# Another issue order for the differential attention, with the second chunk's copy on VectorE

## The reference

```
h   = rms_norm(x);  P = h @ w_in               # split into the q, k, v of two mixers
A   = sliding-window attention, window 128, learned sinks
B   = differential attention: 4 heads, two softmax maps each, chunk-causal over all keys
x   = x + rms_norm(concat(A, B) @ w_out)
x   = x + rms_norm((silu(h2 @ w_gate) * (h2 @ w_up)) @ w_down)

# B, for one block of 128 query rows of one head:
sc = q[m] @ k[m].T / 8, masked;   p[m] = softmax(sc)      # m = 0, 1
o  = (p[0] - lam * p[1]) @ v;     o = rms_norm(o) * g * (1 - lambda_init)
```

## Time and profile before

| what | value |
|---|---|
| median of three runs | 2519.32 us |
| profiled execution, its own time | 2519.68 us |
| its span, first to last instruction | 2517.9 us |
| TensorE busy over the span | 2369.7 us (94%) |
| VectorE, ScalarE, GpSimd busy over the span | 1591.8, 1218.6, 680.0 us |
| B: first score block to last norm | 630.5 to 1015.4 us |

### The profile page before, as it was taken

One profiled execution on the slowest core, in us unless ns is written; L12 is line 12 of the kernel. 1 busy time (PEld: TensorE's weight loads), 2 busy tenths in 40 slices (PEclk: granted clock), 3 DMA queues, 4 the chain that ended last, 5 costly groups with the idle time before them and its releaser, 6 DMA issues.

```text
span 2517.9 us, 34871 instructions
## 1 busy us (share of the span) xinstructions
PE 2369.7 (94%) x11796; PEld 1972.9 (78%) x11796; DVE 1591.8 (63%) x3045; ACT 1218.6 (48%) x2779; POOL 680.0 (27%) x810
## 2 busy tenths in 40 slices
PE   6999987997899999799999999999999999999997
PEld 5888876885778778577778888888888888888886
DVE  5677775554788888333664654657786455465877
ACT  5555564332677777433443333345454333334444
POOL 1233322221576676355511101100001111111001
PEclk9999998998899999899999999999999999999999
DMA  5111112433332231567552322256764332226774
GB/s 172 53 45 55 57 61 84 139 131 111 123 113 71 86 94 35 189 205 256 189 182 103 111 101 101 89 192 227 246 243 140 108 109 97 101 94 247 240 259 142
DMA packets 222354, 340.08 MB, mean 135 GB/s; under 512 B 20577, under 2 KB 119905, under 8 KB 220385
## 3 DMA queue, kind: packets, MB, share of 16 engines
q1 hardware_dynamic: 222176, 337.86, 39.8%
HBM read 234.50 MB, written 103.28 MB: 134 GB/s over the span
## 4 chain that ended last, share of the span: by engine, by line
PE 53%; POOL 2%; DVE 1%; issue 1%; ACT 1%; DMA 1%; SPq 0%; POOLq 0%; DVEq 0%; ACTq 0%
PE ff_psum L2444 33%; PE ff_psum L2468 17%; PE ff_psum L1722 3%; DMA op_w_raw<-in_w_out_dram 1%; PE ff_psum L1736 1%; POOL op_mt_lo L1507 0%; DVE op_h_row L1659 0%; DVE op_y_norm L1651 0%; POOL op_odd L1544 0%; POOL op_odd L1541 0%; ACT op_odd L1606 0%; DMA ff_hop<-hop_s 0%; DVE ff_y L2408 0%; ACT op_w_hi L1621 0%; POOL op_x_rstd L165 0%
## 5 line engine op out<-in xcount | busy, mean ns | idle before, releaser
L2444 PE MATMUL ff_psum<-ff_hop,ff_a_hi 128*128 128x512 f32 x2464 | 760.1, 390 | 3.7 <-DVE ff_hop L2208 2.8
L2444 PEld LDWEIGHTS ff_psum<-ff_hop,ff_a_hi 128*128 128x128 f32 x2464 | 463.0, 188 | 100.5 <-issue 5.0
L2444 PE MATMUL ff_psum<-ff_hop,ff_a_lo 128*128 128x512 f32 x1232 | 480.1, 390 | 0.0
L2444 PEld LDWEIGHTS ff_psum<-ff_hop,ff_a_lo 128*128 128x128 f32 x1232 | 231.6, 188 | 48.4
L2468 PE MATMUL ff_psum<-ff_a_hi 128*128 128x512 f32 x616 | 239.8, 389 | 0.0
L2468 PE MATMUL ff_psum<-ff_a_hi,ff_a_lo 128*128 128x512 f32 x616 | 239.7, 389 | 0.0
L2468 PE MATMUL ff_psum<-ff_a_lo,ff_a_hi 128*128 128x512 f32 x616 | 239.6, 389 | 0.0
L2074 ACT ACTIVATE ff_a_hi<-ff_w_raw 128x512 fp32r<-128x512 f32 x220 | 137.9, 629 | 194.2 <-PE ff_psum L2444 191.2
L2201 DVE TENSOR_TENSOR ff_a_lo<-ff_w_raw,ff_a_hi 128x512 fp32r<-128x512 f32 x220 | 163.4, 745 | 90.4 <-ACT ff_a_hi L2074 90.4
L1207 ACT ACTIVATE da_probs<-da_psum,da_bias 128x512 f32<-128x512 f32 (+3 forms) x320 | 195.7, 624 | 50.8 <-DVE da_bias L1259 45.8
L2029 POOL TENSOR_TENSOR ff_go<-ff_go 128x512 f32<-128x512 f32 x22 | 28.4, 1291 | 655.1 <-DVE ff_go L2282 635.2
(11 more groups left out here) (230 smaller groups left out, 4983.9 us busy)
## 6 DMA issues: line engine op xcount, KB each, us to landing
g_s<-ff_go SPq DMA_DIRECT2D x154, 256.0 KB, 2.0
ff_ring<-g_s SPq DMA_DIRECT2D x154, 256.0 KB, 2.7
ff_ring<-in_w_down_dram SPq DMA_DIRECT2D x132, 256.0 KB, 3.1
ff_w_raw<-in_w_gate_dram SPq DMA_DIRECT2D x44, 512.0 KB, 3.3
ff_w_raw<-in_w_up_dram SPq DMA_DIRECT2D x44, 512.0 KB, 3.4
pp_x<-in_x_dram SPq DMA_DIRECT2D x32, 512.0 KB, 4.3
ff_hop<-hop_s SPq DMA_DIRECT2D x14, 1024.0 KB, 7.8
hop_s<-op_odd SPq DMA_DIRECT2D x8, 1280.0 KB, 5.4
```

The lines of the kernel that those rows point to most:

```text
L2444: last = pe.matmul(ps[:, bank, :], w[:, unit % R, at], hop[i][:, h, c, :], start=(i in (0, 1, 6) and c == 0 and x_ == 0), stop=(c == 3 and ...
```

## The change

Four things differ, all in B. First, the shifts in `KINDS` and the durations that the planner assumes are other numbers; so is what an output scaling P must come after. Second, `COPIED_BY` gives chunk 1 to VectorE (G) in place of ScalarE (H). Third, three heads are planned in place of four, and the order of the third, seams included, is used for every head; events of the second head that fall behind the start of the third are marked as belonging to the head before ("ago" 1). Fourth, the wait of B on the factor is written for chunk 1 by number, which is the same chunk.

```
-    "S": ("PE", (-2.39, -1.12)),
+    "S": ("PE", (-1.33, -1.82)),
...
-COPIED_BY = ("H", "H", "H", "G")
+COPIED_BY = ("H", "G", "H", "G")
...
-    for h in range(DH):
+    for h in range(heads):
...
-                    us=1.85 * part[c] + 0.25 if combine == "A" else 0.98 * part[c] + 0.1)
+                    us=1.75 * part[c] + 0.3 if combine == "A" else 0.56 * part[c] + 0.1)
...
-            add("P", h, s, us=0.3, after=[("V", h, s, n - 1), second_last[0] >= 0 and ("N", *second_last)])
+            add("P", h, s, us=0.25, after=[("V", h, s, n - 1)])
...
-    order = sorted(start, key=lambda e: start[e])
+    begin = start["S", heads - 1, 0, 0, 0]
+    late = {(kind, *rest) for (kind, h, *rest), t in start.items() if h == heads - 2 and t >= begin}
+    order = []
+    for kind, h, *rest in sorted(start, key=lambda e: start[e]):
+        if h == heads - 2 and (kind, *rest) in late:
+            order.append((1, kind, *rest))
+        elif h == heads - 1 and (kind, *rest) not in late:
+            order.append((0, kind, *rest))
...
-            for kind, h, *rest in order:
-                perform(h, kind, *rest)
+            for event in order:
+                if event[0] == 0:
+                    perform(0, *event[1:])
+            for h in range(1, DH):
+                for ago, *event in order:
+                    perform(h - ago, *event)
+            for ago, *event in order:
+                if ago:
+                    perform(DH - 1, *event)
```

More of the change, by code:

```diff
@@ L912 @@
 KINDS = {
-    "S": ("PE", (-2.39, -1.12)),
[L914 to L926, removed]
+    "S": ("PE", (-1.33, -1.82)),
+    "R": ("DVE", (-0.33, 0.02)),
+    "M": ("DVE", (-1.55,)),
+    "E": ("ACT", (1.72, -2.49)),
+    "C": ("DVE", (-2.37,)),
+    "A": ("POOL", (0.0,)),
+    "B": ("DVE", (1.29,)),
+    "T": ("PE", (0.04,)),
+    "H": ("ACT", (0.17,)),
+    "G": ("DVE", (0.17,)),
+    "V": ("PE", (1.59,)),
+    "P": ("DVE", (1.31,)),
+    "Q": ("ACT", (-0.38,)),
+    "N": ("POOL", (1.3,)),
 }
 COMBINED_BY = ("A", "B", "A", "B")
-COPIED_BY = ("H", "H", "H", "G")
+COPIED_BY = ("H", "G", "H", "G")
 def attention_plan():
@@ L939, in attention_plan @@
     steps = len(chunks)
-    hop, own = 0.16, 0.05
+    heads, hop, own = 3, 0.16, 0.06
     events, turns = {}, {kind: [] for kind in KINDS}
@@ L958, in attention_plan @@
                 for c in range(n):
-                    add("S", h, s, m, c, us=max(0.455 * part[c], 0.28) + 0.03, after=[slot("E", "S", S_SLOTS)])
-                    add("R", h, s, m, c, us=0.53 * part[c] + (0.21 if c == n - 1 else 0.13), after=[("S", h, s, m, c)])
-                add("M", h, s, m, us=0.1, after=[("R", h, s, m, c) for c in range(n)])
+                    add("S", h, s, m, c, us=max(0.43 * part[c], 0.32), after=[slot("E", "S", S_SLOTS)])
+                    add("R", h, s, m, c, us=0.53 * part[c] + (0.34 if c == n - 1 else 0.07), after=[("S", h, s, m, c)])
+                add("M", h, s, m, us=0.08, after=[("R", h, s, m, c) for c in range(n)])
                 for c in range(n):
@@ L964, in attention_plan @@
                         after=[("M", h, s, m), second_last[0] >= 0 and ("T", *second_last, chunks[second_last[1]] - 1)])
-            add("C", h, s, us=0.46, after=[("E", h, s, m, c) for m in range(2) for c in range(n)])
+            add("C", h, s, us=0.6, after=[("E", h, s, m, c) for m in range(2) for c in range(n)])
             for c in range(n):
@@ L1009, in diff_attn @@
     ordinal, total = {}, {}
-    for kind, _, *rest in sorted(e for e in order if e[1] == 0):
-        ordinal[(kind, *rest)] = total[kind] = total.get(kind, 0) + 1
+    for _, *e in sorted(order, key=lambda e: (e[2], e[0])):
+        ordinal[tuple(e)] = total[e[0]] = total.get(e[0], 0) + 1
     S_BANKS, T_BANKS, O_BANK = range(S_SLOTS), range(S_SLOTS, S_SLOTS + T_SLOTS), S_SLOTS + T_SLOTS
@@ L1275, in perform @@
                         cols = slice(4 * P * c, 4 * P * c + width(s, c))
[L1276 removed]
+                        if c == 1:
                             dve.wait_ge(factor_ready, h * steps + s + 1)
```

10 lines of the change are left out of this document (5 added, 5 removed).

## The result

The changed kernel takes 2537.61 us (median of 4 runs, 2535.62 to 2540.92) against 2519.50 (2518.02 to 2520.41): ratio 1.0074, 95% interval 1.0056 to 1.0091, 18.1 us slower.

What follows compares the result with a forecast made beforehand. No engine is full: four hand work round in a ring, with 22.5 us of each 93.60 us head GpSimd's alone. 1.2 us a head, 4.8 in all, added to 2519.68 gave 2524.5 us; 8-in-10 range 2515 to 2537.

Steps and rivals of the forecast that it cites:

- B is closed: Attention stage: its gain or loss reaches the kernel one for one; no stage outside changes by more than 0.5 us.
- The sum of 1.2 us a head: Whole head, four times: slip of 1.2 us each, 4.8 in all; own range 0.5 to 2.5, chance 0.45.
- The seam, 0.95: Change of head: N11 ahead of A13 waits for late P11, making A14 0.95 us late; GpSimd keeps it through its stretch.
- Step 6, M6.0 1.2 late: VectorE, step 6: M6.0 moves behind R6.03 and R6.10, starting 1.2 us later, and the exponentials with it.
- Step 7, the copies ahead of M7.1, 1.4: VectorE, step 7: G6.1 and G6.3 add 0.93 us to 0.5, so M7.1 is 1.4 late; C7 slips 1.2.
- Step 8, G7.1 ahead of M8.1: VectorE, step 8: 0.60 us copy makes M8.1, C8 and T8.0 1.8 late; TensorE's saved 0.4 leaves S9.13 1.4 late.
- Steps 9 to 11: Later steps: copies go into VectorE's idle time, TensorE saves some 0.2 us, T11.0 is 1.2 late.
- The copies at nothing: VectorE copies in the GpSimd stretch (G12.1, G13.1, G2.1), or in front of an R waiting for scores, cost nothing.
- B beside A, taken as none: Combinations on VectorE beside A on GpSimd: could cost -0.8 to +0.8 us a step in four steps; taken as none.
- A (the seam absorbs): Rival: GpSimd's stretch starts when it did, losses inside a head vanish; -0.4 to +0.3 us a head, 2519.5 us, chance 0.22.
- B is out: Rival: TensorE's order decides and is faster, 1.3 us a head, 2514.5 us, if C8 slips under 0.5; chance 0.13.
- C, half of the copies pushing: Rival: VectorE becomes the bound; all copies 2545.3 us, half 2532.5; from half upward and what lies between, chance 0.20.

Runs made afterwards that it cites:

- r1: Changed kernel with GpSimd's order of before (A1 ahead of N15, A2 ahead of N0, A13 ahead of N11): 2536.51 us, ratio 1.0077.
- p1: Kernel before with GpSimd's order of after (N15 ahead of A1, N0 ahead of A2, N11 ahead of A13): 2523.19 us, ratio 1.0025.
- f4: Kernel before with the new order only from step 10 over the change of head to step 5, copies on ScalarE: 2525.10 us, ratio 1.0029.
- g2: p1 with two pairs of filler score matmuls on TensorE ahead of S6.02, written to the output bank: 2519.98 us, ratio 1.0010.
- s1: Kernel before with M6.0 alone moved behind R6.10 on VectorE: 2517.99 us, ratio 1.0004.
- r5: Changed kernel with copies G6.1 and G6.3 back behind M7.1, and G7.1 behind M8.1, on VectorE: 2548.28 us, ratio 1.0122.
- f3: Kernel before with the new order only in steps 7 to 9 of each head, copies on ScalarE: 2525.48 us, ratio 1.0030.
- f1: Kernel before with the new order on all engines and steps, chunk 1 copied by ScalarE, copies in chunk order: 2538.00 us, ratio 1.0079.
- e1: Kernel before, old order kept, the 48 copies of chunk 1 executed by VectorE, each in its place: 2528.31 us, ratio 1.0038.
- f2: Kernel before with the new order only from the end of step 5 to step 7, copies on ScalarE: 2526.26 us, ratio 1.0028.
- r2: Changed kernel with V6.1 and V6.2 put back behind S8.03 on TensorE: 2536.19 us, ratio 1.0078.
- r4: Kernel before with T6.3, V6.1 and V6.2 put ahead of S8.01 on TensorE: 2534.31 us, ratio 1.0068.
- x2: Kernel before, copies on ScalarE, with the new order on TensorE and VectorE only: 2572.93 us, ratio 1.0219.

## Why the prediction was wrong

*B is closed.* Right: 20.5 us of stage against 18.1 of time. The bound that I set to the rest, 0.5 us, was too sharp. The part outside the stage reads 2133.0 before, 2132.1 after, and 2128.1 in r1, with the same code there.

*The sum of 1.2 us a head.* This is the step that failed: one of its terms was put at nothing, two have the wrong sign, and the last is too small. The forecast's "0.95 at the seam, 1.4 before it" are two readings of one running slip, which starts at nothing and is 0.95 when A14 comes round again. Head 2 of the changed kernel has no low stretch and loses 98.0 - 93.6 = 4.4. Read the same way, with each event's lateness against the kernel before, it divides so:

| from | to | forecast | measured |
|---|---|---|---|
| A14 | A5 | 0 | 1.11 |
| A5 | T8.0 | 1.8 | 2.24 |
| T8.0 | T11.0 | -0.6 | 0.53 |
| T11.0 | next A14 | -0.25 | 0.53 |
| all | | 0.95 | 4.41 |

The largest part of the error stands in the three rows that I put at nothing or at a gain.

*The seam, 0.95.* "GpSimd keeps it through its stretch", and the copies "cost nothing" there. A14 was judged nearly rightly: 0.6 late against the first score, and in p1 not late at all. But I never walked steps 0 to 5, where T13.0's wait reaches S0.10 and N15 and N0 stand ahead of A1 and A2 (A1 2.5 late). f4, seam and steps 0 to 5 together, measures 2.0. GpSimd's own order is 0.9 of it in the old kernel (g2: 94.5) and 0.4 in the new; the other engines make the rest.

*Step 6, M6.0 1.2 late.* In the changed kernel it is 1.2 later than A5, as said, on top of A5's 1.7. As a cause it is small: s1, with 0.60 us of R in front of M6.0 in the old order, costs 0.2.

*Step 7, the copies ahead of M7.1, 1.4.* Right in size, wrong as a cause. R7.12 is 2.1 late and M7.1 2.9, so the copies put 0.8 on it, and r5 takes 0.8 off. But C7, which I let follow from it, waits behind R8.01 for S8.01, and r5 shows that in this order of TensorE the copies have to stand there.

*Step 8, G7.1 ahead of M8.1.* G7.1 was counted. S8.01 behind three values was not: R8.01 waits 2.06 us for it, which makes C7 and A7.0 late and TensorE stand still for 2.39 us ahead of T7.0. Nor was P6 ahead of R8.03, which holds two R for V6.3 and costs f3 its 1.9 us a head; in the changed kernel the first wait hides it.

*Steps 9 to 11.* I expected TensorE to win here; the slip grows from 3.9 (T8.0) to 4.5 (T11.0). Which move makes it no run shows.

*The copies at nothing.* In the new order nearly right: f1, less an estimated 1.5 us for its low stretch, is 97.5 a head, after 98.0. In the old order it is wrong (e1, 2.6 a head). So what they cost depends on their slots in an order and is no fixed share of VectorE's time.

*B beside A, taken as none.* 6.1 us of VectorE's time more in the stage; what it costs in the end no run tells apart.

*The clock.* Not in the forecast at all: 1.5 us in each of two heads, 3.0. The kernel before pays for one low stretch too, in head 0: 1.0 us, if p1's head 0 with it (92.9) and g2's without (91.9) are set side by side. That leaves 2.0 of the 20.5. The earlier trace rows had 0.98 for the whole stage and the row after 0.97; a mean like that hides stretches of 3 us.

*The rivals.* A (the seam absorbs) is right for A14 in p1 and wrong for the kernel. B is out: C8 slips 3.9. C, half of the copies pushing, gave 2532.5 and was the nearest rival in number, by the wrong cause: f1 has ScalarE make the copies and is no faster. Its last reading, that the 79 ns between the two copies are a dearer access of PSUM on VectorE, doesn't hold either. By shape, before, VectorE's copy takes 280 ns for 128 columns and 680 for 512, ScalarE's 274 and 601, so the difference is in the columns. The Trainium skill, in "Perfetto Trace Analysis" under Identifying the Most-Contended Engine, would have the engine of the highest occupancy be the one to relieve first. VectorE is the fullest here, at 349.5 of 406 us against 292.5 of TensorE's weight loads. Relieving it by 48 copies changed nothing in the new order (f1), while in the old one the same copies on it cost 10.4 us (e1). So in this ring of four engines at 64 to 86% the rule doesn't say what the relief is worth.

How the 20.5 us divide, as an estimate from single profiles: the lower clock 2.0; the copies 0.5 a head, 2.0; GpSimd's order 0.4 a head, 1.4; the remaining 15 the order of TensorE, VectorE and ScalarE together. Of this, three parts of a head are shown to cost something when they alone are put into the old order: steps 5 to 7 (f2), steps 7 to 9 (f3) and from step 10 over the change of head to step 5 (f4). Single instructions are shown only in part: P6 in f3, N11 and N15 in p1, the values ahead of S8.01 in the changed kernel by its trace and by r2. Which moves make the rest stays open. No version was found that beats the kernel before.

## What to carry to other kernels

Where several engines hand work round at 65 to 85% each, follow one running slip through the whole loop body, the steps that look unchanged too, and take nothing off it unless a row shows the idle time that absorbs it. When a single move gives nothing back, look for a second obstacle that it uncovers (r2, f3). Price a moved instruction by who stands behind it on its own engine and by whether what it waits for was moved as well: r4, r5 and x2 each change one side only and cost 3 to 14 us a head. Where TensorE gets a new standstill, here of 1.16 and 2.39 us, look at the clock of the stretch behind it, repetition by repetition, and not at the mean.
